# A convolution chunk's taps divided between VectorE and TensorE in the attention mixer

## The reference, cut to what matters

```python
p = h @ w_in[l]
attn = mla_group(...)                     # 8 heads, softmax over chunk-causal scores
u = a * jax.nn.sigmoid(g)                 # conv_group: 512 channels
y = lax.conv_general_dilated(u, conv_w, window_strides=(1,), padding=[(30, 0)],
                             feature_group_count=512) + conv_b
conv = jax.nn.silu(layer_norm(y, ln_g, ln_b))
x = x + jnp.concatenate([attn, conv], axis=-1) @ w_out[l]
```

## Time and profile before

| | us |
|---|---|
| median of three runs | 2464.78 (2464.42 to 2466.94) |
| profiled execution | 2465.07 |
| its span | 2463.4 |
| mean granted TensorE clock | 0.977 of 2.4 GHz |
| TensorE busy | 2392.7 (97% of the span) |
| VectorE busy | 1898.9 |
| ScalarE busy | 1441.3 |
| GpSimd busy | 16.2 |

### The profile page before, as it was taken

One profiled execution on the slowest core, in us unless ns is written; L12 is line 12 of the kernel. 1 busy time (PEld: TensorE's weight loads), 2 busy tenths in 40 slices (PEclk: granted clock), 3 DMA queues, 4 the chain that ended last, 5 costly groups with the idle time before them and its releaser, 6 DMA issues.

```text
span 2463.4 us, 33422 instructions
## 1 busy us (share of the span) xinstructions
PE 2392.7 (97%) x12180; PEld 2016.4 (82%) x12180; DVE 1898.9 (77%) x1945; ACT 1441.3 (59%) x1488; POOL 16.2 (1%) x34
## 2 busy tenths in 40 slices
PE   8999998999999999999999989998999999998998
PEld 8888897888888888888888778886888888867887
DVE  8766677889898989898989776678666766696765
ACT  4544445777777777777777654445544544555543
POOL 1000000000000000000000000000000000000000
PEclk9999998999999999999999989997999999997999
DMA  7555553999999999999999945542455555432552
GB/s 269 181 187 187 189 171 121 362 348 365 348 365 347 365 348 365 348 364 349 362 349 366 349 138 187 188 148 86 137 188 187 179 188 187 160 127 86 183 188 90
DMA packets 83240, 594.44 MB, mean 241 GB/s; under 512 B 9468, under 2 KB 9500, under 8 KB 11996
## 3 DMA queue, kind: packets, MB, share of 16 engines
q1 hardware_dynamic: 81216, 587.76, 66.0%
q0 software_dynamic: 1520, 4.40, 0.6%
q10 hardware_dynamic: 432, 1.31, 0.1%
HBM read 592.38 MB, written 1.05 MB: 241 GB/s over the span
## 4 chain that ended last, share of the span: by engine, by line
PE 91%; DVE 6%; ACT 1%; issue 1%; DMA 1%; DVEq 0%; SPq 0%; ACTq 0%
PE banks L1047 17%; PE banks L1098 9%; PE banks L1100 9%; PE banks L1104 9%; PE banks L1049 8%; PE banks L1123 8%; PE banks L1125 8%; PE banks L1124 8%; PE banks L1076 2%; PE banks L1349 2%; DVE lo L1623 2%; DVE acc L2058 1%; PE banks L1220 1%; PE banks L1139 1%; PE banks L1379 1%
## 5 line engine op out<-in xcount | busy, mean ns | idle before, releaser
L1623 DVE TENSOR_TENSOR lo<-raw,hi 128x2048 fp32r<-128x2048 f32 x550 | 1258.4, 2289 | 221.2 <-ACT hi L561 217.7
L561 ACT CAST hi<-raw 128x2048 fp32r<-128x2048 f32 x550 | 1051.7, 1913 | 266.0 <-PE banks L1104 129.7
L1047 PE MATMUL banks<-xhl,hi 128*128 128x512 f32 x1776 | 632.0, 400 | 0.7 <-DVE lo L1623 0.4
L1049 PE MATMUL banks<-xhl,lo 128*128 128x256 f32 x1776 | 499.8, 281 | 0.0
L1047 PEld LDWEIGHTS banks<-xhl,hi 128*128 128x128 f32 x1776 | 335.0, 189 | 84.3 <-DVE lo L1623 2.0
L1123 PE MATMUL banks<-hi,xhl 128*128 128x512 f32 x896 | 354.5, 396 | 0.8 <-issue 0.8
L1125 PE MATMUL banks<-hi,xhl 128*128 128x512 f32 x896 | 350.4, 391 | 0.0
L1124 PE MATMUL banks<-lo,xhl 128*128 128x512 f32 x896 | 349.6, 390 | 0.0
L1098 PE MATMUL banks<-hi,hh 128*128 128x512 f32 x872 | 343.9, 394 | 1.8 <-DVE hl L1635 1.8
L1100 PE MATMUL banks<-lo,hh 128*128 128x512 f32 x872 | 341.4, 392 | 0.0
L1049 PEld LDWEIGHTS banks<-xhl,lo 128*128 128x128 f32 x1776 | 337.1, 190 | 1.9
(11 more groups left out here) (357 smaller groups left out, 2425.1 us busy)
## 6 DMA issues: line engine op xcount, KB each, us to landing
raw<-in_moe_w_gate SPq DMA_DIRECT2D x112, 1024.0 KB, 4.9
raw<-in_moe_w_up SPq DMA_DIRECT2D x112, 1024.0 KB, 4.9
raw<-in_moe_w_down SPq DMA_DIRECT2D x112, 1024.0 KB, 4.9
raw<-in_ffn_w_gate SPq DMA_DIRECT2D x58, 1024.0 KB, 4.9
raw<-in_ffn_w_up SPq DMA_DIRECT2D x58, 1024.0 KB, 4.8
raw<-in_ffn_w_down SPq DMA_DIRECT2D x58, 1024.0 KB, 4.8
raw<-in_mix_pieces SPq DMA_DIRECT2D x46, 1024.0 KB, 4.9
raw<-in_mix_pieces SPq DMA_DIRECT2D x2, 768.0 KB, 4.0
```

The lines of the kernel that those rows point to most:

```text
L561: nc.scalar.copy(hi[:, hslot(S, c), 0:n], raw[:, c % RING, 0:n]).then_inc(S.hi_done, 1)
L1047: pe.matmul(bank[b + s][:, :], hi[:, hr, a:a + P], xhl[:, k, :], start=(k == 0), stop=False, skip_group_check=True)
L1049: mm = pe.matmul(bank[b + s][:, 0:T], lo[:, r, a:a + P], xhl[:, k, 0:T], start=False, stop=(k == KD - 1), skip_group_check=True)
L1623: v.tensor_tensor(lo[:, c % RING, 0:n], raw[:, c % RING, 0:n], hi[:, hslot(S, c), 0:n].bitcast(F32), ALU.subtract).then_inc(S.lo_done, 1)
```

## The change

Of chunk 3's 30 taps that VectorE made, taps 1 to 14 stay there (with ScalarE's first that is 15), and taps 15 to 30 go to TensorE: for each, a 128x128 matrix with the tap's 128 numbers on its diagonal is multiplied with the shifted 256 columns of `upad`, and the sixteen products add up in bank 5. GpSimd makes the sixteen matrices (`diag`) from the identity once x is complete ahead of the mixer; they lie over the feed-forward buffers. TensorE has 3, 3, 3, 3, 2 and 2 products at the end of steps 2 to 7 of the loop over heads, the first behind waits for chunk 3's gate and for the matrices. VectorE adds bank 5 to `acc` at the end. q's groups 1 and 3 exchange their banks, so that bank 5 is written last, and the wait for `small_read` moves from ahead of group 0 to ahead of group 3. VectorE's taps are given out anew.

```diff
+CK_V = 15
+        diag = nc.alloc_sbuf_tensor_at("diag", [P, CK - CK_V, P], F32, offset=nc.sbuf_base)
-        Q_BANKS = ((4, 6), (5, 7))
+        Q_BANKS = ((4, 6), (7, 5))
...
-            pe.wait_ge(ev("small_read"), l + 1)
             for n, (h, t) in enumerate(HALVES):
+                if n == 3:
+                    pe.wait_ge(ev("small_read"), l + 1)
...
+                if 2 <= i < NH:
+                    if i == 2:
+                        pe.wait_ge(ev("gate_out"), 8 * (l + 1))
+                        pe.wait_ge(ev("diag_made"), (CK - CK_V) * (l + 1))
+                    for k in range(CK_V + (0, 3, 6, 9, 12, 14)[i - 2], CK_V + (3, 6, 9, 12, 14, 16)[i - 2]):
+                        mm = pe.matmul(bank[R_BANK][:, 0:T], diag[:, k - CK_V, :], upad[:, 3, k:k + T],
+                                       start=(k == CK_V), stop=(k == CK - 1))
+                    if i == NH - 1:
+                        mm.then_inc(ev("conv_mm"), 1)
...
+                pool.wait_ge(x_done, 4 * st["M"])
+                for k in range(CK_V, CK):
+                    g.tensor_scalar(diag[:, k - CK_V, :], ident[:, :], col(("cw2", l), 4 * k + 3), None,
+                                    ALU.mult).then_inc(ev("diag_made"), 1)
...
-                done, tap_at, ready = [1] * 4, [0] * 4, [0, 1, 2]
+                done, tap_at, ready, end = [1] * 4, [0] * 4, [0, 1, 2], (CK, CK, CK, CK_V)
-                        left = [c for c in chunks if done[c] < CK]
+                        left = [c for c in chunks if done[c] < end[c]]
-                conv(20, ready)
+                conv(16, ready)
-                    conv((3, 3, 2, 8, 2, 8, 8, 8)[h], ready)
+                    conv((4, 2, 2, 6, 3, 6, 6, 6)[h], ready)
                 conv(200, ready)
+                dve.wait_ge(ev("conv_mm"), l + 1)
                 settle()
-                mark(ev("conv31_out"))
+                v.tensor_tensor(acc[:, 3, :], acc[:, 3, :], bank[R_BANK][:, 0:T], ALU.add).then_inc(ev("conv31_out"), 1)
```

More of the change, by code:

```diff
@@ L1589, in _ @@
             load_gain(1)
-            for g in range(2):
-                pool.wait_ge(ev("xg_done"), TT * (g + 1))
-                load_gain(2 + g)
-                B = next(st["B"] for st in stages if st["kind"] == "mix2" and st["layer"] == g)
-                pool.wait_ge(main.multiplied, B + 9)
+            for l in range(2):
+                pool.wait_ge(ev("xg_done"), TT * (l + 1))
+                load_gain(2 + l)
+                st = next(st for st in stages if st["kind"] == "mix2" and st["layer"] == l)
+                pool.wait_ge(x_done, 4 * st["M"])
+                for k in range(CK_V, CK):
+                    g.tensor_scalar(diag[:, k - CK_V, :], ident[:, :], col(("cw2", l), 4 * k + 3), None,
+                                    ALU.mult).then_inc(ev("diag_made"), 1)
+                pool.wait_ge(main.multiplied, st["B"] + 9)
                 pool.dma_start(qkT[QK:KEYS, :, :], hide).then_inc(ev("mask_in"), 16)
```

## The result

The changed kernel takes 2448.91 us (median of 4 runs, 2447.94 to 2450.59) against 2465.86 for the kernel before beside it (2464.42 to 2466.94): ratio 0.9932, 95% interval 0.992 to 0.9943. The profiled executions are 2448.98 (span 2447.3) and 2465.07 (span 2463.4), 16.1 us apart. In the changed file TensorE's lines of the mixer stand 2 to 3 lower down (the products are L1471), VectorE's 17 or 18 (maxima L2209, taps L2075, low part L1640).

A forecast was written before the change was run, and what follows sets the result against it. VectorE's dependent taps were taken to break TensorE's matmul stream in the head loop. Per layer 4.5 + 1.1 + 0.7 + 0.4 - 0.5 = 6.2 us, twice 12.4, from 2465.07, median 0.3 lower: 2452.5 us; range 2449.5 to 2459.5.

The forecast's parts named there:

- What bounds it, and the clock among the heads: Head loop: VectorE's dependent taps delay each head's maxima; after the change TensorE's clock stays at 2.4 GHz.
- rival B: Head loop: early gaps bring one clock fall, pushing heads 2 and 3 back 1 to 2 us per layer; 2455 to 2457; chance 0.10.
- The nine taps: Head 2's to head 7's maxima: 19 taps instead of 28, 0.505 us each, save 4.5 us per layer.
- The four taps ahead of the heads: VectorE ahead of head 0: removing four taps gains nothing, since VectorE already waits 2.40 us for the first scores.
- the term for q's order: q's products: waiting only ahead of the last group starts TensorE 0.4 us sooner per layer, bounds 0 to 0.6.
- The tail: Behind head 7's maxima, at 2.4 GHz: 1.1 us saved to attention's end, then 0.7 us to the first output product.
- GpSimd: Mixer start: sixteen diagonal multiplications of 0.28 us may disturb VectorE; cost 0.5 us per layer, bounds 0 to 1.2.
- rival C: Mixer start: GpSimd holds VectorE up 1.2 us, a longer L1085 gap lowers the clock, 1.7 us more; 2457.5; chance 0.12.
- A: Head loop: clock stays at 1.2 GHz, so TensorE's products make it slower, 4.9 us per layer; 2474.6; chance 0.06.
- D: Head loop: taps were not what the heads waited for, or ScalarE is next; 2464; chance 0.06.

The follow-up runs named there:

- taps apart: Changed kernel with every second of the fourth chunk's last consecutive taps written to the first chunk's sum instead (result differs): 2448.0 us.
- all taps and q's old order: Kernel before plus the 16 diagonal matrices and products, result unused; VectorE keeps all 31 taps, old pacing and old bank order of q: 2465.11 us, ratio 0.9996.
- q's order: Kernel before with only q's new bank order and the `small_read` wait moved ahead of the last group: 2465.08 against 2465.77 us, ratio 0.9996.
- four taps alone: Kernel before with only four taps moved from ahead of the key outputs (16 for 20) into VectorE's wait for head 0's scores: 2463.53 us, ratio 0.9987.
- four taps in VectorE's wait: Changed kernel with four taps moved from among the heads into VectorE's wait for head 0's scores: 2444.63 us, ratio 0.9913.

## Why the prediction was right in sign and low in size

**What bounds it, and the clock among the heads: right.** VectorE's taps bounded the heads: taking them away alone brings 23.7 us there, with or without the products. TensorE runs at 2.4 GHz from 1698.1 to 1718.6; four products take 1.95 us and three 1.51, so 0.44 each where 0.434 was said. The first three ran at 1.2 GHz (2.91 us), the small form of rival B, but VectorE was at its taps and its low part meanwhile. Head 3's maxima come 0.2 us later behind head 2's than before, the low part (1697.06) having waited 0.14 us for ScalarE's high part.

**The nine taps: count right, price low by 0.8 us.** The step that failed is "eight dependent taps took 4.04, 0.505 each, so the nine save 4.5". A tap that follows on the same sum starts 0.52 us after it, one in turn with another chunk 0.40. Nine fewer is 9 x 0.52 = 4.7. But seven of those that stay had also been dependent and now stand in turn, as the pacing leaves five of chunk 2's taps for the heads: 7 x 0.125 = 0.9. That is 5.6, less 0.2 by which head 3's maxima come later: 5.3 measured (21.87 to 16.54). The kernel with the taps apart shows the price of the order by itself. The same goes for heads 0 and 1, which were to stay as they are: three dependent taps at head 1 became two in turn, and a cheap one was added at head 0, 0.4 us in all.

**The four taps ahead of the heads: wrong, and the largest miss in one place.** "Worth nothing there: VectorE already waits 2.40 us for the first scores". The wait was real, but it stood behind a chain that the taps had delayed. Behind its block of taps VectorE reads bank 5 and the keys out of PSUM, and where the clock stays up TensorE waits for both: 1.84 us for bank 5 ahead of q in the kernel with all taps and q's old order, 0.17 with four taps fewer; 1.08 us for the keys with q's new order. So TensorE is not "gapless to the first scores" either, as the term for q's order had it. A wait at the end of a chain doesn't make the work at its start free. In the table, M0 by taps in that block, order of q, and clock beside q (set that fell to 1.2 GHz or stayed at 2.4):

| taps | q | stayed | fell |
|---|---|---|---|
| 20 | old | 68.2 (products, all taps) | 67.95 (before, both), 68.2 |
| 20 | new | 67.4 (q's order) | 67.6 (q's order), 67.8, 67.9 |
| 16 | old | 66.3 (four taps alone), 66.6 | 67.5 (four taps alone) |
| 16 | new | 66.1 (changed, layer 0) | 67.8 (changed, layer 1) |

Two chains end at M0. With 20 taps VectorE's is the longer one and the clock hardly matters. With 16 it is TensorE's, which is 1.7 us longer if the clock falls. (The kernels with GpSimd's work have 0.1 to 0.3 of it in every number; without that work, 16 taps and the new order with the fall give 67.7, no better than the old order.) So the four taps earned 1.3 us on top of q's order in layer 0 of the profile and nothing in layer 1. The same instructions in the same order had the fall in one layer and not in the other, which may be why its runs spread over 2.7 us; the unprofiled ones don't show it.

**The tail: first part right, second given back.** Head 7's maxima to the reciprocal: 1.04 saved, 1.1 forecast. To the first output product 0.70 in layer 0, 0.7 forecast, 0.33 in layer 1. But the clock fell at 1718.6 and 2223.8, for 3.4 us each, over the turns and the first output products, and the stretch behind is 0.69 and 0.42 longer. The second term is thus worth nothing in either layer. The sum had no term for a new fall behind the heads, though rows 4 show TensorE waiting 1.67 us ahead of the turns there. The wait alone doesn't decide it: it is as long in the kernel with four taps in VectorE's wait, where the clock stayed up, and why it fell here stays open.

**q's order: right** (0.4 forecast; 0.36 to 0.58 and 0.5 in the two comparisons; the weights of the first L1404 are loaded at 1671.34, 0.43 us behind those of the product before).

**GpSimd: price of one instruction wrong, effect too high.** 0.60 us each in place of 0.28, and 0.15 to 0.2 us on the path in place of 0.5. The rule of the Trainium skill (SBUF — State Buffer, Who interferes with whom) is that a VectorE instruction with two SBUF inputs and a GpSimd one that reads SBUF exclude each other, and that the order of issue decides who is held; by this, the prediction said, the cost would be at its upper bound. The trace agrees with one half: a multiplication that begins behind VectorE's low part is held until that has ended (2.39 and 2.42 us in place of 0.60). It doesn't agree with the other: the low part that began while a multiplication was running took 2.34 us in place of 2.28, where a hold to the multiplication's end would have cost 0.43. So the price fell on the engine that had time, and rival C fell with it. Its half about TensorE, that a longer gap at rb would bring the clock down, was not put to the test (the wait is 1.26 in place of 1.11). Its sum is also 0.3 us off: 3.8 per layer give 2457.2, not 2457.5.

**The sum again.** Forecast 6.2 per mixer; measured terms in layers 0 and 1: M0 1.8 and 0.2, heads 5.7 and 5.7, tail 1.05 and 0.95; 8.6 and 6.8, together 15.4 where 12.4 was said. By terms, the heads gave 2.4 us more than forecast over both layers, M0 2.2 more, and the tail 1.6 less. Part of M0's is luck: 1.7 of it hangs on the fall beside q, which layer 0 of the profile was spared and layer 1 was not. The remaining 0.7 of the 16.1 lies outside the mixers. Layer 0's x is complete 1.1 us earlier already (1622.13 against 1623.26), and part of that goes again later. This is chance and not the change: all 17 profiled kernels run the same program up to there, and x is complete between 1622.1 and 1625.6.

Rivals A and D fall with the first paragraph. The range failed at its near end: its lower bound took every known term at its best and had no room for a term wrongly set to zero.

## What to carry to other kernels

A wait in front of an instruction shows slack of that instruction, not of the work ahead of it on the same engine: follow what that work releases before calling its removal free. When work moves from a bounding engine to an idle one, count also the order in which the remaining instructions follow one another, and give the idle engine so much that the two pace each other; here 15 and 16 of 31 did, while 23 on VectorE lost 13 us and 7 won nothing. A clock that is kept up is worth what runs at it on the path, so look where it will fall next.

## What the runs showed of the hardware

- VectorE's 128x256 multiply-and-add lasts 0.48 us in the record. It starts 0.395 us after the last one if that wrote another chunk's sum ((2.46 - 0.48) / 5) and 0.52 us after if it reads that one's result ((3.08 - 0.48) / 5).
- GpSimd's 128x128 multiplication by a column takes 0.60 us, and 2.39 or 2.42 where it begins while VectorE's low part combines two SBUF tiles of 128x2048 (2.34 and 2.38 us). Beside it VectorE's instructions are a little longer: 2.28 to 2.34 and 2.38, nine taps 4.65 to 5.02, a 128x128 one 0.28 to 0.33.
- Twenty products of 2 columns (2.29 us) ahead of full ones were followed by 3.4 us at 1.2 GHz in 15 of 30 profiled layers; with 32 columns they took 2.31 us, and none of the four profiled layers that have them shows it. Whether the width is the cause is open.
